# Beginning the output map inside the mixers: a Trainium2 kernel for four transformer layers

## The reference

```python
for l in range(DEPTH):                      # layers A, DEPTH = 2
    ya, yb, yc = swa(...), fox(...), mlstm(...)            # 512 + 256 + 256 columns
    x = x + jnp.concatenate([ya, yb, yc], axis=-1) @ w_out  # the output map
    u = _rms(x, norm2) @ w_ff1
    x = x + jnp.square(jax.nn.relu(u)) @ w_ff2
for l in range(DEPTH):                      # layers B
    mix = jnp.concatenate([o_sb, o_mla, o_rwkv], axis=-1) @ w_o   # 256 + 256 + 512 columns
    x = layer_norm(DEEPNORM_ALPHA * x + mix, ln1_g, ln1_b)
    u_act, u_gate = jnp.split(x @ ffn_w_up, 2, axis=-1)
    ...
```

## Time and profile before

| | us |
|---|---|
| median of 3 runs (lowest, highest) | 3115.62 (3115.13, 3124.98) |
| the profiled execution's own time | 3116.76 |
| its span, first to last instruction | 3114.9 |
| PE busy | 2850.8 (92%) |
| PE weight loads busy | 2342.8 (75%) |
| DVE busy | 1484.7 (48%) |
| ACT busy | 991.7 (32%) |
| POOL busy | 191.6 (6%) |
| mean granted clock of TensorE, of full speed | 0.943 |

### The profile page before, as it was taken

The page is one execution under the profiler, slowest core; times in us unless marked ns, Lnnn a source line. Parts: engine busy times, 40 slices in busy tenths (PEclk is TensorE's granted clock), DMA queues, the critical chain, the costliest instruction groups (busy, mean ns, idle before and its releaser), DMA issues.

```text
span 3114.9 us, 45264 instructions
## 1 busy us (share of the span) xinstructions
PE 2850.8 (92%) x20012; PEld 2342.8 (75%) x20012; DVE 1484.7 (48%) x2296; ACT 991.7 (32%) x1494; POOL 191.6 (6%) x182
## 2 busy tenths in 40 slices
PE   7998999999998999999868789999998787799998
PEld 5876888878777888887548668888876487578887
DVE  3555443444464444334464564443633555554445
ACT  3334322232333322223342233233332422232322
POOL 0200000001100000000013300000000123100000
PEclk9988999999989999999879889999999788899999
DMA  4101222222003222221000023232210000222221
GB/s 169 55 1 64 95 95 95 95 73 104 14 1 109 106 95 97 98 95 41 0 1 30 3 107 125 92 108 87 95 54 14 0 3 30 82 95 96 101 89 67
DMA packets 30868, 216.59 MB, mean 70 GB/s; under 512 B 3664, under 2 KB 3920, under 8 KB 6224
## 3 DMA queue, kind: packets, MB, share of 16 engines
q1 hardware_dynamic: 30672, 213.69, 19.5%
HBM read 211.58 MB, written 2.10 MB: 69 GB/s over the span
## 4 chain that ended last, share of the span: by engine, by line
PE 83%; DVE 11%; ACT 3%; issue 1%; DMA 0%; DVEq 0%; SPq 0%; ACTq 0%
PE PS L538 76%; PE PS L541 3%; PE PS L698 2%; DVE SC L1274 2%; DVE R L1274 1%; DVE SM L1274 1%; ACT SPL L2025 1%; ACT LN L2025 1%; DVE X L1282 1%; DVE SPL L1274 1%; DVE HA L1274 1%; DVE SM L1285 1%; PE PS L1101 1%; PE PS L1051 1%; PE PS L692 0%
## 5 line engine op out<-in xcount | busy, mean ns | idle before, releaser
L538 PE MATMUL PS<-H,SPL 128*128 128x512 f32 (+1 forms) x4560 | 1053.5, 392 | 17.2 <-DVE SPL L1274 10.7
L538 PEld LDWEIGHTS PS<-H,SPL 128*128 128x128 f32 (+1 forms) x4560 | 850.8, 187 | 202.7 <-issue 13.1
L1274 DVE TENSOR_TENSOR SPL<-RAW,SPL 128x2048 fp32r<-128x2048 f32 (+2 forms) x194 | 433.9, 2240 | 728.9 <-ACT SPL L2025 728.8
L2025 ACT ACTIVATE SPL<-RAW 128x2048 fp32r<-128x2048 f32 (+2 forms) x194 | 361.4, 1868 | 872.6 <-PE PS L538 829.9
L538 PE MATMUL PS<-SPL,Uu 128*128 128x512 f32 x2592 | 589.8, 389 | 0.0
L538 PEld LDWEIGHTS PS<-SPL,Uu 128*128 128x128 f32 x2592 | 486.5, 188 | 101.0
L538 PE MATMUL PS<-SPL,H 128*128 128x512 f32 (+2 forms) x2112 | 460.8, 380 | 25.7 <-DVE SPL L1274 25.0
L538 PEld LDWEIGHTS PS<-SPL,H 128*128 128x128 f32 x2112 | 387.4, 192 | 98.6 <-issue 27.1
L2025 ACT ACTIVATE R<-PS 128x512 f32<-128x512 f32 (+2 forms) x162 | 93.0, 584 | 203.4 <-PE PS L538 177.0
L2025 ACT ACTIVATE Uu<-R 128x512 fp32r<-128x512 f32 x108 | 68.3, 632 | 141.0 <-DVE R L1274 141.0
L1274 DVE TENSOR_TENSOR Uu<-R,Uu 128x512 fp32r<-128x512 f32 x108 | 74.8, 693 | 79.5 <-ACT Uu L2025 79.5
(11 more groups left out here) (230 smaller groups left out, 2588.1 us busy)
## 6 DMA issues: line engine op xcount, KB each, us to landing
RAW<-in_wA SPq DMA_DIRECT2D x84, 1024.0 KB, 4.8
RAW<-in_wB SPq DMA_DIRECT2D x84, 1024.0 KB, 4.9
RAW<-in_wAo SPq DMA_DIRECT2D x8, 1024.0 KB, 4.8
RAW<-in_wBo SPq DMA_DIRECT2D x8, 1024.0 KB, 5.0
LN<-in_ln SPq DMA_DIRECT2D x4, 1024.0 KB, 5.9
P<-in_pB SPq DMA_DIRECT2D x2, 1920.0 KB, 8.4
RAW<-in_wBm SPq DMA_DIRECT2D x4, 704.0 KB, 4.0
X<-in_x SPq DMA_DIRECT2D x4, 512.0 KB, 5.6
```

What stands on the lines that cost most here:

```text
L538: return pe.matmul(out, l_, r_, start=start, stop=stop)
L1274: return v.tensor_tensor(out, a, b, o)
L2025: return a.activation(out, in_, f, scale=scale)
```

## The change

1. **First weights split in the mixers.** In A, group 11 goes to slot 1, which is free when strand 2 has ended (`first_split`: ACT waits for `at_y[2]`, then one high and one low part of 128 x 2048). In B, group 12 goes to a fourth slot, `U[7168:9216]` and `L2` (memory of `R` and `LN`, free when `post` of tiles 0 and 1 is done, `first_split_b`), and ACT splits group 13 at the end of the mixers. Scratch tiles of tiles 0 and 1 (`wide01`) change places for this, and the squares of `post` go to `XT` instead of `QT`.
2. **Transposes of the heads first.** The 32 transposes become 16 and 16 (`turned_y`). In B the first 16 (stick-breaking and latent heads) stand in the mixers behind the scan (`joint`), followed by three of the four token tiles of the first weight group (`out_tile(0)` to `out_tile(2)`, 12 products each). In A the first 16 come behind the fence, then `out_tile(0)`, the other 16, and the rest.
3. **One fence less** per layer: the second is gone.
4. **Gates and the bonus.** Tiles 2 and 3 take their gate in banks 4 and 6, waiting for `po_a` only. POOL begins its part of `post` when the last product of `prep` is done (`pr_q`), not behind the scan's output (`sc_y`).
5. **SP.** In B the loads of `LN` and `P` come after the fourth weight group of the output map (was: after the second), and wait also for the first group's products.

```diff
@@ split_plan
-        if i in (first_group(2) + 12, first_group(3) + 12):
-            turn = 0
+        if i in (first_group(0) + 11, first_group(1) + 11):
+            ring, turn = [1, 2, 0], 0
+        elif i in (first_group(2) + 4, first_group(3) + 4):
+            ring, turn = [0, 1], 0
+        elif i in (first_group(2) + 12, first_group(3) + 12):
+            first, ring, turn = [3], [1, 0, 2], 0
@@ slot
+            if slot_of[i] == 3:
+                return U[:, 7168:9216], L2[:, 0:2048]
@@ tensor
+            def turned_y(src, chunks, banks):
+                for c, b in zip(chunks, banks):
+                    for t in range(4):
+                        ins = tr(bank(b)[:, t * 128:(t + 1) * 128], src(c, t))
+                    ins.then_inc(s.ht, 1)
+            def out_tile(b):
+                i = at["group"]
+                hi, lo = slot(i)
+                if b == 0:
+                    pe.wait_ge(s.lo, i + 1)
+                sl = slice(b * 128, (b + 1) * 128)
+                for k in range(4):
+                    ah, al = from_h2(k) if b == 0 else h2(k)
...
@@ post (tensor)
-                if t:
-                    pe.wait_ge(s.po_z, 4 * l + t)
-                mm(bank(1), GD[:, t * 128:(t + 1) * 128], par(PB, P, "g2")).then_inc(s.po_g, 1)
+                if t == 1:
+                    pe.wait_ge(s.po_z, 4 * l + 1)
+                elif t:
+                    pe.wait_ge(s.po_a, 4 * l + t + 1)
+                mm(bank((1, 1, 4, 6)[t]), GD[:, t * 128:(t + 1) * 128], par(PB, P, "g2")).then_inc(s.po_g, 1)
+            def joint(l):
+                while ("states", 3) not in flags:
+                    yield
+                at["h2"] = n("h2", 8) - 8
+                pe.wait_ge(s.sc_k, 6 * l + 6)
+                pe.wait_ge(s.po_z, 4 * l + 2)
+                turned_y(lambda c, t: YB[:, t, c * 128:(c + 1) * 128], range(4), sets[0])
+                for b in range(3):
+                    yield
+                    out_tile(b)
@@ layers A (tensor)
-                transposed(lambda c, t: YA[:, t, c * 128:(c + 1) * 128], None)
-                fence()
-                dense(l, (l, "out"), of_h2)
+                turned_y(lambda c, t: YA[:, t, c * 128:(c + 1) * 128], range(4), sets[1])
+                out_tile(0)
+                turned_y(lambda c, t: YA[:, t, c * 128:(c + 1) * 128], range(4, 8), sets[1])
+                for b in range(1, 4):
+                    out_tile(b)
+                out_rest((l, "out"))
+                chunk((l, "out", 1), 2, of_h2, "T", sets[1], freed=by_add)
@@ scalar
+            def first_split(l):
+                while ("at", 2) not in flags:
+                    yield
+                a.wait_ge(s.at_y[2], len(UNITS_A[2]) * (l + 1))
+                high_part(first_group(l) + 11)
+            def joint(l):
+                while ("states", 3) not in flags:
+                    yield
+                high_y(range(4), sets[0])
+                high_part(first_group(2 + l) + 13)
@@ gpsimd, post
-                g.wait_ge(s.sc_y, 4 * l + t + 1)
+                g.wait_ge(s.pr_q[t], 9 * l + 9)
@@ sync
-                    if i == first_group(2 + l) + 14:
-                        whole(6 + 3 * l + 2)
+                    if i == first_group(2 + l) + 16:
+                        whole(4 + 2 * l + 2)
+                        sp.wait_ge(s.mm, used_at[first_group(2 + l) + 12])
```

More of the change, by code:

```diff
@@ L157, in split_plan @@
         while len(slot) < min(i + n, allowed[i]):
-            sl = turn % n
-            turn = sl + 1
+            if first:
+                sl = first.pop()
+            else:
+                sl = ring[turn % len(ring)]
+                turn += 1
             todo.append(len(slot))
@@ L1242, in tensor @@
                 turns(latent(l), stick_, strand(2, UNITS_B[2]), strand(3, UNITS_B[3]), features(l),
-                      *[prep(l, t) for t in range(4)], scan(l), *[post(l, t) for t in range(4)])
+                      *[prep(l, t) for t in range(4)], scan(l), *[post(l, t) for t in range(4)], joint(l))
                 fence()
-                transposed(lambda c, t: YB[:, t, c * 128:(c + 1) * 128], None)
-                fence()
-                dense(2 + l, (2 + l, "out"), of_h2, tiles=True)
+                turned_y(lambda c, t: YB[:, t, c * 128:(c + 1) * 128], range(4, 8), sets[1])
+                out_tile(3)
+                out_rest((2 + l, "out"))
+                by_tiles((2 + l, "out", 1), of_h2, sets[1], (4, 4), by_add)
                 n("lns")
@@ L1266, in vector @@
             beside = []
-            at = {"group": 0, "owed": 0}
+            at = {"group": 0, "owed": 0, "split": 0}
             def own(ins):
@@ L1672, in mixer_a @@
                 flags.clear()
-                turns(head(l), *[strand(i, UNITS_A[i], lag=2 * i) for i in range(3)])
+                turns(head(l), *[strand(i, UNITS_A[i], lag=2 * i) for i in range(3)], first_split(l))
             def latent_norm(l):
@@ L1894, in post @@
                 v.wait_ge(s.n_sq, 8 + 4 * l + t + 1)
[L1895 removed]
+                own(red(var, rk["XT"][t].rearrange("p (h d) -> p h d", h=8), ALU.add))
                 ts(var, var, 1.0 / 64, 64e-5, ALU.mult, ALU.add).then_inc(s.n_ss, 1)
@@ L1984, in vector @@
                 turns(latent(l), stick_, strand(2, UNITS_B[2]), strand(3, UNITS_B[3]), features(l),
-                      *[prep(l, t) for t in range(4)], scan(l), *[post(l, t) for t in range(4)])
+                      *[prep(l, t) for t in range(4)], scan(l), *[post(l, t) for t in range(4)], first_split_b(l),
+                      joint(l))
                 fence()
-                transposed()
-                fence()
+                low_part(first_group(2 + l) + 13)
+                low_y(range(4, 8), sets[1])
                 dense((2 + l, "out"), ALPHA, "ln")
@@ L2418, in post @@
                 yield
+                flags["post", t] = True
                 yield
@@ L2516, in scalar @@
                 turns(latent(l), stick_, strand(2, UNITS_B[2]), strand(3, UNITS_B[3]), features(l),
-                      *[prep(l, t) for t in range(4)], scan(l), *[post(l, t) for t in range(4)])
+                      *[prep(l, t) for t in range(4)], scan(l), *[post(l, t) for t in range(4)], first_split_b(l),
+                      joint(l))
                 fence()
-                transposed()
-                fence()
+                high_y(range(4, 8), sets[1])
                 dense("ln")
```

123 lines of the change are left out of this document (90 added, 33 removed).

## The result

Four runs of the changed kernel took 3077.99, 3078.01, 3085.01 and 3093.33 us, a median of 3081.51; four of the kernel before on the same chip had a median of 3120.3. The ratio is 0.9864, with a 95% interval of 0.9827 to 0.9901, so between 31 and 54 us less; 50.4 were forecast from the profiled execution. The change makes the kernel faster, and the forecast of 3065 is 16 to 21 us too low for a typical run: the median of the first four lies inside its range of 3053 to 3085, the mean of all sixteen 1.4 us outside.

What follows compares the result with a forecast made beforehand. PE's waits and work were taken as the bound, with DVE's normalisation in `post` in B. Gains of 10.1 (A ends), 38.7 (B ends) and 1.6 (earlier B) sum to 50.4 us: 3065 predicted, range 3053 to 3085.

Steps and rivals of the forecast that it cites:

- the four ends: Ends of the mixers in two layers A and two layers B: gains of 10.1 and 38.7 us together.
- The meeting 2.7 later: Layers A: the remaining fence at the mixers' end comes 2.7 us later because the weight split stands before it.
- 50.0 from transposes to X: Layers A: PE's stretch from the first 16 transposes behind the fence to the transposes of X takes near 50 us.
- the meeting 1.2 later: Layers B: the fence at the mixers' end comes 1.2 us later, bounds -1.6 and +5.
- the even chance for the clock: Layers B, early products: after PE's 4.1 us idle, higher or lower clock equally likely; the lower costs 2.2 us.
- the forecast's own signs of being wrong: PE waiting for weights or `LN` in the output map, DVE over 1 us for a gate, PE for POOL in `prep`.
- rival 1: Layers B: late high and low parts delay early tiles and gates, fence 8.6 us later, 3080 us in all; chance 0.13.
- rival 2: `prep` in B: POOL and DVE exclude each other, low part costs 2.5 us a layer, 3075 in all; chance 0.10.
- POOL's early start for tiles 0 and 1: Layers B: POOL's part of `post` moves ahead, gaining 0.8 us a layer, between 1.6 gained and 1.6 lost.
- no effect: Rival 4: the mixers' end slips as much as PE gains, 3115 us; chance 0.03.
- slower: Rival 5: the clock stays at the lower level through the output maps, 3240 us; chance 0.03.
- more: Rival 3: the split in A lies beside idle time and the clock never falls in B, 3055 us; chance 0.08.

Runs made afterwards that it cites:

- Experiment 7: Changed kernel with the layers A's first weight split moved behind the fence: ratio 0.9915 to the kernel before; with that split's low part on POOL instead: 0.9905.
- experiment 3: Changed kernel with POOL's part of `post` again waiting for `sc_y` instead of `prep`'s last product: ratio 0.9859 to the kernel before.
- experiment 4: Changed kernel with PE's gates of tiles 2 and 3 ahead of the early products: ratio 0.9867 to the kernel before; also with first high and low parts earlier: 0.982.
- experiment 6: Experiment 4's kernel with both edits, plus group 14's load held until DVE has subtracted tile 2's mean in `post`: ratio 0.9852 to the kernel before.

## Why the prediction was right, point by point

The forecast was right in its direction, in the four ends that it worked out, and in its range; one cost that it did not have was made good by something that the runs do not name, and that part is luck (see the sum).

**Layers A.** The meeting 2.7 later: 2.59 measured. 50.0 from transposes to X: 48.93 and 49.93. I had counted the lower clock once at 2.2; in the first layer the 12 early products took 3.19 for 2.73 and the transposes 3.67 for 1.91, together 2.2 as well, and no wait for a low part shows. The gain came out at 6.4 and 5.7 for 5.3 and 4.8 because I had added up durations that overlap: the four rows behind the meeting sum to 49.85 and last 48.93. Experiment 7 shows that the split inside the mixers, priced at 2.7, buys 3.0 and 4.7.

**Layers B, behind the meeting.** 37.4 forecast, 37.25 in both layers of all three profiles; weights, `LN` and `P` cost nothing, as taken.

**Layers B, ahead of it.** This is the term that was mis-sized: the meeting 1.2 later, measured 2.98 and 2.19 (2.14 to 3.31 over the three profiles). The pieces were right one by one: DVE's two operations short (experiment 3), roots at +9.4 behind the first `SC<-R,PS` where I had +10.0, first early product at +6.9 where I had +6.9. What failed is the even chance for the clock. The forecast set an idle time of 4.1 against a fall of the clock 5.4 behind PE's last product. By its own rows the fall came 5.0 behind it (1782.13 to about 1787.1), and in the changed kernel it came 2.5 behind PE's last transpose, which ends at 1795.04:

```profile
1797.00:1798.00 1.00, 0.00 (x0) 0.00 (x0) 0.96 (x3) 1.00 (x3) 0.00 (x0) 0.76 0.00 0
```

The lower level came in every profile of the changed kernel (24 products took 7.2 to 8.3 for the 5.5 forecast and the 5.8 of experiment 4), and the gates stand behind them, so that DVE waited 0.65 to 1.79 for the gate of tile 2. A wait above 1 us there was one of the forecast's own signs of being wrong, and it stands in two of the six ends. That is rival 1 in small, a quarter to a third of its 8.6. Experiment 4 parts the two causes: the order alone gave 1.9 in the second layer, and order and clock together 2.8 in the first.

Two readings of the earlier trace rows were loose. The forecast set DVE's 1.01 beside 0.36 for "two of the same kind", but those are operations with two inputs, and the 1.01 is one with a constant and one input tile. Its single time is 0.17, so the excess is 0.84 and the sum of 1.6 stands. What the forecast cites on two SBUF inputs bears on the 1.49, not on the 1.01.

**Earlier in B, the split.** The low part of group 12 was costed at 0 with a bound of 2.5. The collision came as rival 2 had it (2.50 became 4.28), but PE did not feel it (experiment 6). The Trainium skill (GPSIMD Engine Reference, Key points) names contention with VectorE instructions of two SBUF inputs; here the low part's two inputs are both in SBUF, and it is POOL that waits while DVE takes its usual 2.28. What the first layer did lose, 1.4 to 1.8, came from the load that the split sets free, which I had looked at for its landing and not for what runs beside it. POOL's early start for tiles 0 and 1 (0.8 a layer forecast) stays unresolved. From DVE's last `R<-R,PS` of tiles 0 and 1 to the first of tiles 2 and 3 the kernel of experiment 3 took 59.6 and 62.3 in the two layers, the three profiles of the changed kernel 59.0 to 59.6 and 59.9 to 63.5.

**Earlier in B, the slots.** The forecast has no term for the new turn of the two slots, and so puts it at nothing. It costs PE 5.5 us of waiting in the first layer B in every profile, and the stretch there is 12.5 to 16.8 longer than in the one profile of before.

**The sum.** 48.8 of the 50.4 lay in the four ends, and 48.5 were found there. That they meet so closely is in part luck too: A gained 12.1 for 10.1 and B 36.4 for 38.7. Less the 12.5 to 16.8 of the first layer B that would leave 32 to 36. The plain means gave 43.7, give or take 7. So the forecast's total is nearer than its terms deserve. What makes up the difference stays open: the stretch of before may usually be longer than in its one profile (that execution, at 3116.76, was 13 us faster than the mean of the 45), or the changed kernel gains by a higher clock elsewhere. For the same reason the forecast's starting point was low, and 3065 with it. The rivals: "no effect" and "slower" fell, "more" did not come since the clock fell in B each time.

## What to carry to other kernels

Work that is moved ahead of a meeting into another engine's queue is worth its place only if it is fed at once: 4 us of waiting in front of it cost the clock as well, and putting one short ready piece (here two gates, 1.9 us) into that gap gave back 2.8 and 1.9. When a buffer is freed earlier, ask which transfer that starts and what code runs beside it. When the turn of a ring of buffers is changed, write down for each use who had the buffer before: one group behind its direct predecessor cost 5.5 us of PE, far from the place of the change. Before two kernels are compared over a stretch, find its first and last instruction in each of them, since the same clock time is another piece of work. And where a run's time follows its mean clock as closely as here, compare single stretches in the trace, or times at equal clock, before small edits are judged by medians.

## What the runs showed of the hardware

A load of 1 MB beside the small matmuls of `prep` cost PE 1.35 to 1.79 us in the first layer B in all nine profiles that had it at the first level, without any semaphore in it, and nothing in the second, though the burst is the same (DMA share 0.97 and 0.95 in these windows of 2 us of the changed kernel); behind the last level it was mostly the second layer whose stops were longer, by about 2, though stops of 2.37 are there once without the load:

```profile
1756.00:1758.00 2.00, 2.00 (x73) 2.00 (x70) 1.32 (x2) 0.26 (x1) 0.61 (x2) 1.00 0.97 410
...
2624.00:2626.00 2.00, 2.00 (x73) 2.00 (x70) 1.20 (x2) 0.38 (x1) 0.60 (x2) 1.00 0.95 401
```

That PE waited for its own instructions, which come over the same DMA engines (the page has a queue of instructions with 158 packets), fits this and was not shown; single stops up to 1.66 marked "issue" are there without any such load too. The mixers' clock is a draw: the mixers of the second layer A ran in 119.6, 126.7 and 141.4 us in three profiles of the same program, at 0.93, 0.87 and 0.76.
